# One block for all phases of a hybrid HGRN2 and gated-delta-net layer: a counted border, and three projection parts issued ahead of it

## The chip, the cores and the metric

The kernel runs on one core of a Trainium2 chip. The metric is the device time of one execution in microseconds (us), from start to end of the program. The kernel before takes 740.03 us, the median of three runs.

## What is computed

One decoder layer on 16 learned meta tokens and 1024 tokens of width 1024, in float32. In short:

```python
u = rmsnorm(h, norm_w)
proj = einsum('btd,dc->btc', u, w_in)           # 4096 columns + 8 gate columns
o_hg = causal_mixer(hgrn2_chunk, (q, k, v, logf), S0)              # 4 heads of 128
o_gd = causal_mixer(gdn_chunk, (gq, gk, gv, g, beta), S0g)         # 4 heads of 128, after a causal convolution of width 4
y = concatenate([gated_rmsnorm(o_hg, z_hg), gated_rmsnorm(o_gd, z_gd)])
h = h + einsum('btc,cd->btd', y, w_out)
out = rmsnorm(h, final_norm_w)[:, 16:]
```

`hgrn2_chunk` is a gated linear recurrence with a decay for each channel; `gdn_chunk` solves a lower triangular system in each chunk and carries a state from chunk to chunk.

## The kernel before, in words

**Tokens and heads.** The tokens are padded to 9 chunks of 128, in three groups g of three chunks. The normalised, transposed input stays in SBUF as a high and a low part (`uTh`, `uTl`), and each weight tile of 128 columns is split in the same way (`w_high` by ScalarE, `split_high`, L260; `w_low` by GpSimd, `split_low`, L268). A projection takes three products for each of 8 slices of the inner dimension.

**Phases.** The program runs nine phases: `front` (norm, transposes, gates and the first projection), then for every head h a delta-net phase `phase_gd(h)` (called gd0 to gd3 here) and an HGRN2 phase `phase_hg(h)` (hg0 to hg3). Each is a block of its own (`with nc.Block() as block`, L367, L1042, L1703), in which every engine has its own instruction stream. At the end of a block all engines meet at a barrier, and `end_block` (L192) clears the semaphores; the next phase uses the other half of them.

**The projection runs one step ahead.** While a phase works on its own head, TensorE projects what the next phase needs, so that TensorE always has work. A projection phase has 4 weight tiles of 3 token pieces, 12 pieces in all, and each piece is 8 parts (`project_part`, L241): 96 parts of three matmuls, numbered from 0. The steps of a phase each get some parts by a table (`give` in `phase_gd`, `parts` in `phase_hg`), and TensorE issues them behind the step's own matmuls. In hg3 the parts are those of the output product instead (`out_part`, L1099; 16 pieces of 6 parts, three matmuls of 512 columns each). Piece i is complete at part 8i+7, so piece 8 ends with part 71 and piece 10 with part 87.

**Who reads the table.** ScalarE, GpSimd and VectorE find their work on a piece by the step in whose parts the piece ends (`pieces`). ScalarE copies the piece out of PSUM (`take_hg`, L1715; `take_gd`, L1260), and behind pieces 2, 5 and 8 it splits the next weight tile. GpSimd does the low part at the same step in the gd phases:

```python
for key in order:
    ...
    take_low(pool, parts[key])            # pieces 2, 5, and 8 if more phases follow
    if key == ("blocks", 1):
        pool.wait_ge(m_in, 16)
        for g in range(NG):
            expand(pool, M, blk_m, g).then_inc(m_set, 1)
```

The steps of a gd phase are A1, A2 and A3 for each group (parts 0 to 31), `("blocks", 0)` (parts 32 to 41), `("blocks", 1)` (42 to 69), then for levels i = 4, 5, 6 `("B1", i)` with 3 parts and `("B2", i)` with 4, and `("end",)` with the last 5. Behind `("blocks", 1)` comes level 4: TensorE forms the product Y, ScalarE copies it, TensorE does the 3 parts of B1, and then forms Z = M Y (L2043), for which it waits for `m_set`, the three expansions of M by GpSimd (L1781). SyncE issues the weight tile that the third split of a gd phase needs (`load_weights(sp, 3, ...)`) behind the block moves of the triangular solve, `blk_m` among them.

In an hg phase the steps are `lead`, eight `gram` steps for each group, the `t` and `ty` steps at the end of a group (transposes), `rec` steps (the recurrence) and `end`. Transposing a group's normalised output (`ty`, L1606) waits for ScalarE's `normalise` (L1340) of that group. For the last group this is `turned`: it stands before the last part but one of `end` (L1638), and behind it only two parts are left.

Of the kernel before, what the change touches and what calls it, by code (L numbers as in the profile page):

```python
# [32 lines left out]
F32 = mybir.dt.float32  # L33
# [69 lines left out]
def hybrid_layer(nc, x, meta_tokens, norm_w, w_in, conv_w, lb_logits, hg_norm_w, A_log, dt_bias,  # L103
# [87 lines left out]

    def end_block():  # L192

        nonlocal mix_full, mix_free, raw_loaded, w_high, w_low, last_stored, piece_done, piece_out, eps_added
        nums = [s.num for s in sems.values()]
        nc.sync.sem_clear(range(min(nums), max(nums) + 1))
# [44 lines left out]
    def project_part(pe, n, kind, early=0):  # L241
# [10 lines left out]
        for k in range(part * per, (part + 1) * per):  # L252
            for i, (w, u) in enumerate(((wh, uh), (wh, ul), (wl, uh))):
                last = pe.matmul(acc[:, 0:tw], w[j % 2][:, k, :], u[:, k, t0:t0 + tw],  # L254
                                 start=(k == 0 and i == 0), stop=(k == KT - 1 and i == 2))
        if part == PARTS - 1:
            last.then_inc(piece_done, 1)

# [108 lines left out]
    with nc.Block() as block:  # L367
        x_in, rows_in, gate_in = [sem(f"x_in{i}") for i in range(XS)], sem("rows_in"), sem("gate_in")
        gate_high, gate_low, gate_done, gate_out = (sem(n) for n in ("gate_high", "gate_low", "gate_done", "gate_out"))
        const0, consts = sem("const0"), sem("consts")  # L370
        sq_done, rstd_done, scaled = sem("sq_done"), sem("rstd_done"), sem("scaled")
        cleared, u_high, ident_there = sem("cleared"), sem("u_high"), sem("ident_there")
        u_low = [sem("u_low_dve"), sem("u_low_pool")]
        lb_step, lb_exp = sem("lb_step"), sem("lb_exp")
        prm_in, blk_set = sem("prm_in"), sem("blk_set")
        ones_set, pm0, gate_step, mask_step, mask_set = sem("ones_set"), sem("pm0"), sem("gate_step"), sem("mask_step"), sem("mask_set")
        gate_exp, dec_sub, dec_exp = (sem(n) for n in ("gate_exp", "dec_sub", "dec_exp"))
        gam_stored, dec_in = sem("gam_stored"), sem("dec_in")
        tap0, conv_step, conv_done, silu = sem("tap0"), sem("conv_step"), sem("conv_done"), sem("conv_silu")

        @block.sync
        def _(sp):
            def load_x(i):
                sp.dma_start(xt[i % XS][:, :], x[0, (i - 1) * P:i * P, :]).then_inc(x_in[i % XS], 16)

            def load_tile(n, cols_):

                if n >= 2:
                    sp.wait_ge(w_low, n - 1)
                sp.dma_start(raw[(n - 1) % 2][:, :, :], cols_).then_inc(raw_loaded[(n - 1) % 2], 16)  # L390

            sp.dma_start(xt[0][0:META, :], meta_tokens).then_inc(x_in[0], 16)
            load_x(1)
            sp.wait_ge(cleared, 1)
            sp.dma_start(rows[0:48, :], conv_w.rearrange("l j (b c) -> (l j b) c", c=P)).then_inc(rows_in, 16)
            sp.dma_start(rows[48:56, :], norm_w.rearrange("l (b c) -> (l b) c", c=P)).then_inc(rows_in, 16)
            sp.dma_start(rows[56:64, :], lb_logits.rearrange("l (b c) -> (l b) c", c=P)).then_inc(rows_in, 16)
            sp.dma_start(rows[64:65, :], hg_norm_w).then_inc(rows_in, 16)
            sp.dma_start(rows[65:66, :], gdn_norm_w).then_inc(rows_in, 16)
            for i in range(2, XS):  # L400
                load_x(i)
            sp.dma_start(gate_raw[:, :, :], w_in_v[:, :, AB_COLS:AB_COLS + 2 * HEADS]).then_inc(gate_in, 16)
            for i in range(XS, NC):
                full(sp, front, ("x", i - XS, 1))
                load_x(i)
            load_tile(0, tile_cols("gd", GD_KINDS[0], 0))
            sp.dma_start(pr[:, 0, :], A_log[0:1, :].broadcast_to([P, HEADS])).then_inc(prm_in, 16)
            sp.dma_start(pr[:, 1, :], dt_bias[0:1, :].broadcast_to([P, HEADS])).then_inc(prm_in, 16)
            load_tile(1, tile_cols("gd", GD_KINDS[1], 0))
            load_tile(2, tile_cols("gd", GD_KINDS[2], 0))  # L410
            load_tile(3, tile_cols("gd", GD_KINDS[3], 0))
            load_tile(4, tile_cols("hg", 0, 0))
            freed(sp, front, "gam_rows")
            sp.dma_start(gam_dram, gamT[:, :]).then_inc(gam_stored, 16)
            sp.wait_ge(gam_stored, 16)
            load_decay(sp, 0, dec_in)
            load_tile(5, tile_cols("hg", 1, 0))
            sp.wait_ge(raw_loaded[0], 48)

        def rows_of(i):  # L420

            return META if i == 0 else P

        def low_part(eng, n):
# [3 lines left out]
            eng.wait_ge(u_high, n + 1)  # L428
            eng.tensor_tensor(ul[:, 4 * half:4 * half + 4, t0:t0 + w],
                              ut[n % 3][:, 0:4 * w].rearrange("p (k t) -> p k t", k=4),  # L430
                              uh[:, 4 * half:4 * half + 4, t0:t0 + w].bitcast(F32),
                              ALU.subtract).then_inc(u_low[n % 2], 1)

        @block.gpsimd
        def _(pool):
            pool.memset(neg_half[:, :], -0.5)
            pool.memset(ident[:, :], 0.0).then_inc(const0, 1)
            pool.memset(tri[:, :], 1.0).then_inc(const0, 1)
            pool.wait_ge(const0, 2)
            pool.affine_select(out=ident[:, :], in_=ident[:, :], compare_op=ALU.not_equal, fill=1.0,  # L440
                               base=0, pattern=[[-1, P]], channel_multiplier=1).then_inc(const0, 1)

            pool.affine_select(out=tri[:, :], in_=tri[:, :], compare_op=ALU.is_ge, fill=0.0,
                               base=0, pattern=[[1, P]], channel_multiplier=-1).then_inc(const0, 1)
            pool.wait_ge(const0, 4)
            pool.tensor_copy(mask_st[:, 0, :], ident[:, :]).then_inc(consts, 1)
            pool.memset(ones[:, :], 1.0).then_inc(ones_set, 1)
            pool.memset(pmask[:, :], 1.0).then_inc(pm0, 1)
            pool.wait_ge(pm0, 1)

            pool.affine_select(out=pmask[:, :], in_=pmask[:, :], compare_op=ALU.is_ge, fill=0.0,
# [33 lines left out]
            for i in range(AHEAD):  # L485
                rstd_tile(i)
# [1635 lines left out]
```

## Time and profile before

| | |
|---|---|
| median of 3 runs | 740.03 us (739.78 to 741.06) |
| profiled execution, device time | 739.73 us |
| its span, first to last instruction | 738.0 us |
| TensorE busy | 710.0 us, 96% of the span |
| VectorE, ScalarE, GpSimd busy | 449.6, 304.3, 350.5 us |
| mean granted TensorE clock | 0.996 of full speed |
| DMA | 44.94 MB, mean 61 GB/s |

All times of the trace are of one execution, whose device time is 1.7 us above its span. "Busy" of TensorE counts from a matmul's start to its modelled end, so that neighbours overlap: how fast TensorE goes is read from start to start. A name in brackets behind a row tells what ended the idle time before it; PEq, SPq and so on are the sequencers of the engines, POOL is GpSimd, DVE is VectorE, ACT is ScalarE, SP is SyncE, and PE is TensorE.

### The profile page before, as it was taken

What the parts mean: (1) busy time and instruction counts of PE and PEld (TensorE: products, weight loads), DVE (VectorE), ACT (ScalarE), POOL (GpSimd) and SP (SyncE); (2) the same over time, 40 slices, a digit from 0 to 9 for tenths busy, and PEclk for the clock granted to TensorE, in tenths of its full rate; (3) what the DMA queues carried; (4) which work ended last, traced back from release to release, by engine and by line L of the source; (5) the groups of instructions that cost most, each with busy time, mean ns of one, the idle gap of its engine ahead of it and who ended that gap; (6) DMA issues with size and microseconds to landing.
All of it is one profiled execution on the core that took longest, in us unless ns stands there. A gap on an engine that the chain in (4) does not pass through costs nothing. (4 is left out here: it accounts for less than half of the span.)

```text
span 738.0 us, 13493 instructions
## 1 busy us (share of the span) xinstructions
PE 710.0 (96%) x4852; PEld 678.4 (92%) x4852; DVE 449.6 (61%) x1017; ACT 304.3 (41%) x798; POOL 350.5 (47%) x462
## 2 busy tenths in 40 slices
PE   7999999999999999999999999999999999999995
PEld 6799999989999999999999999999999998788884
DVE  6854356379882562798924625989336158776247
ACT  6635423624553316345344154445442342232333
POOL 5782342167553322566624323767243456756423
PEclk9999999999999999999999999999999999999998
DMA  8355333130204226531548142102253324211005
GB/s 264 36 63 79 29 36 73 28 50 9 40 26 72 40 47 57 27 32 22 46 44 66 43 63 28 30 9 48 51 89 127 84 77 161 79 56 45 29 23 206
DMA packets 63990, 44.94 MB, mean 61 GB/s; under 512 B 17438, under 2 KB 59044, under 8 KB 63924
## 3 DMA queue, kind: packets, MB, share of 16 engines
q1 hardware_dynamic: 63924, 44.07, 33.3%
q8 instruction: 40, 0.66, 0.4%
q14 instruction: 26, 0.21, 0.1%
HBM read 35.82 MB, written 7.65 MB: 59 GB/s over the span
## 5 line engine op out<-in xcount | busy, mean ns | idle before, releaser
L254 PE MATMUL proj<-uTh,w_high 128*128 128x352 f32 (+4 forms) x768 | 261.3, 340 | 2.4 <-PEq L1703 2.4
L254 PE MATMUL proj<-uTh,w_low 128*128 128x352 f32 (+4 forms) x768 | 245.7, 320 | 0.0
L254 PE MATMUL proj<-uTl,w_high 128*128 128x352 f32 (+4 forms) x768 | 245.2, 319 | 0.0
L254 PEld LDWEIGHTS proj<-uTh,w_high 128*128 128x128 f32 x768 | 145.1, 189 | 3.3 <-issue 3.1
L254 PEld LDWEIGHTS proj<-uTl,w_high 128*128 128x128 f32 x768 | 145.1, 189 | 0.0
L254 PEld LDWEIGHTS proj<-uTh,w_low 128*128 128x128 f32 x768 | 144.2, 188 | 0.0
L272 POOL TENSOR_TENSOR w_low<-w_raw,w_high 128x256 fp32r<-128x256 f32 (+1 forms) x54 | 71.0, 1316 | 87.3 <-ACT w_high L264 40.0
L1221 POOL TENSOR_TENSOR f_suffix<-f_suffix,f_prefix 128x192 f32<-128x192 f32 x84 | 56.5, 672 | 34.0 <-DVE f_prefix L1429 27.2
L1623 PE MATMUL mix<-level_x 128*128 128x128 f32 x448 | 64.1, 276 | 1.1 <-DVE level_x L1420 0.8
L1623 PEld LDWEIGHTS mix<-level_x 128*128 128x128 f32 x448 | 60.5, 191 | 4.7 <-issue 2.8
L1439 DVE COPY_PREDICATED hg_scores<-mask_st,mix 128x384 f32<-128x384 uint8 (+1 forms) x96 | 52.0, 542 | 19.6 <-PE mix L1623 19.2
L1466 DVE SCALAR_TENSOR_TENSOR conv_out<-conv_in,hg_taps,conv_out 128x352 f32<-128x352 f32 (+2 forms) x81 | 50.9, 629 | 0.5
L1429 DVE TENSOR_TENSOR f_prefix<-f_prefix 128x192 f32<-128x192 f32 x84 | 48.0, 572 | 4.3 <-POOL f_suffix L1221 3.7
L1420 DVE TENSOR_TENSOR level_x<-hg_q,f_prefix 128x192 f32<-128x192 f32 (+1 forms) x84 | 48.2, 574 | 2.5
L1213 POOL TENSOR_TENSOR level_x<-hg_k,f_suffix 128x192 f32<-128x192 f32 (+1 forms) x72 | 45.4, 631 | 8.6 <-PE mix L1623 6.5
L876 ACT ACTIVATE gd_o<-mix,gd_cc 128x128 f32<-128x128 f32 x32 | 11.7, 366 | 74.4 <-DVE gd_r L866 74.4
L1109 PE MATMUL proj<-uTh,w_high 128*128 128x512 f32 x96 | 41.2, 429 | 0.7 <-PEq L1703 0.7
L1109 PE MATMUL proj<-uTh,w_low 128*128 128x512 f32 x96 | 37.9, 394 | 0.0
L1109 PE MATMUL proj<-uTl,w_high 128*128 128x512 f32 x96 | 37.8, 394 | 0.0
L2021 DVE COPY_PREDICATED gd_n<-mask_ts,mix 128x384 f32<-128x384 uint8 (+1 forms) x24 | 13.1, 546 | 39.0 <-PE mix L2043 38.4
L264 ACT CAST w_high<-w_raw 128x1024 fp32r<-128x1024 f32 x27 | 28.2, 1044 | 7.9 <-DMA w_raw<-in_w_in 6.7
L1201 POOL MEMSET f_suffix<- 128x384 f32 x12 | 5.7, 474 | 46.5 <-POOLq L1703 46.3
(301 smaller groups left out, 1381.4 us busy)
## 6 DMA issues: line engine op xcount, KB each, us to landing
w_raw<-in_w_in SPq DMA_DIRECT2D x32, 512.0 KB, 8.4
x_tile<-in_x SPq DMA_DIRECT2D x8, 512.0 KB, 6.6
w_raw<-y_scratch SPq DMA_DIRECT2D x8, 384.0 KB, 4.4
decay<-gamma_scratch SPq DMA_DIRECT2D x4, 576.0 KB, 3.7
landing<-in_w_out SPq DMA_DIRECT2D x4, 512.0 KB, 7.8
landing<-in_x SPq DMA_DIRECT2D x3, 512.0 KB, 6.4
out_y<-landing SPq DMA_DIRECT2D x3, 512.0 KB, 2.6
y_scratch<-gd_y SPq DMA_DIRECT2D x6, 192.0 KB, 1.8
```

Of the source, the lines that this page charges most:

```text
L254: last = pe.matmul(acc[:, 0:tw], w[j % 2][:, k, :], u[:, k, t0:t0 + tw], start=(k == 0 and i == 0), stop=(k == KT - 1 and i == 2))
L264: act.copy(wh[n % 2][:, :, :], raw[(n - 1) % 2][:, :, :]).then_inc(w_high, 1)
L272: last = pool.tensor_tensor(wl[n % 2][:, ks, :], raw[(n - 1) % 2][:, ks, :], wh[n % 2][:, ks, :].bitcast(F32), ALU.subtract)
L1109: last = pe.matmul(pbank[idx % 2][:, :], y[t % 2][:, k, :], wo_half(w, k, half), start=(k == 0 and i == 0), stop=(k == OUT_K - 1 and i == 2))
L1213: pool.tensor_tensor(xv_[:, :, 0, :], kv_[:, :, 0, :], sv_[:, :, 0, :], ALU.mult).then_inc(x_even, 1)
L1221: pool.tensor_tensor(sv_[:, :, 0, :], sv_[:, :, 0, :], pv_[:, :, 1, b - 1:b].broadcast_to([P, GW // (2 * b), b]), ALU.mult).then_inc(suf_d ...
L1420: dve.tensor_tensor(xv_[:, :, 1, :], qv_[:, :, 1, :], pv_[:, :, 1, :], ALU.mult).then_inc(x_odd, 1)
L1429: dve.tensor_tensor(pv_[:, :, 1, :], pv_[:, :, 1, :], pv_[:, :, 0, b - 1:b].broadcast_to([P, GW // (2 * b), b]), ALU.mult).then_inc(pre_do ...
L1439: dve.copy_predicated(A[g % 2][:, GC - n:GC, :], mask_st[:, m, :].unsqueeze(1).broadcast_to([P, n, P]), src).then_inc(bank_free(plan, ("gr ...
L1466: dve.scalar_tensor_tensor(out=out_, in0=cin[idx % 3][:, tap:tap + tw], scalar=cw[:, tap, kind:kind + 1], in1=out_, op0=ALU.mult, op1=ALU. ...
L1623: last = pe.matmul(ap[:, chunk(i)], left, right, start=True, stop=True)
L2021: dve.copy_predicated(part3(dst[:, gs]), msk.unsqueeze(1).broadcast_to([P, GC - lo, P]), src).then_inc(bank_free(plan, ("Z", i, g)), 1)
```

## The change

All phases now stand in one block. A semaphore `border` is never cleared; at the end of a phase each engine but TensorE drains and adds one to it (`leave`), TensorE's count is carried by a matmul, and at the start of a phase each engine waits until all five have counted (`meet`). TensorE issues three parts of the next phase's projection (`LEAD = 3`) before its own wait, and the first matmul of them carries its count. Every table of parts starts at 3 instead of 0, and the last step of each phase has three parts less. `clear_old` clears the old half of the semaphores in the next phase.

```diff
+    whole = ExitStack()
+    block = whole.enter_context(nc.Block())
+    border = ctx.enter_context(nc.semaphore("border", num=SEM_LO + 2 * SEM_HALF))
+    ENGINES, LEAD = 5, 3
+    old = []
+    def meet(eng):
+        if phase[0]:
+            eng.wait_ge(border, ENGINES * phase[0])
+    def leave(eng):
+        eng.drain().then_inc(border, 1)
+    def clear_old(sp):
+        if old:
+            sp.sem_clear(range(min(old), max(old) + 1))
...
+                if met is not None and n == 0 and k == 0 and i == 0:
+                    last.then_inc(met, 1)
...
+    def lead_in(pe, kind, low):
+        pe.wait_ge(w_low, low)
+        pe.wait_ge(piece_out, 4 * len(PIECES) - 1)
+        for n in range(LEAD):
+            project_part(pe, n, kind, met=border)
...
+    def out_lead_in(pe, low):
+        pe.wait_ge(w_low, low)
+        pe.wait_ge(piece_out, 4 * len(PIECES) - 1)
+        for n in range(LEAD):
+            out_products(pe, n, met=border)
...
-        parts, at = {}, 0
+        parts, at = {}, LEAD
         for key in steps:
-            n = {"lead": 4, "end": 10}.get(key[0], 4 if key[:2] == ("rec", NG - 1) else 2)
+            n = {"lead": 4, "end": 10 - LEAD}.get(key[0], 4 if key[:2] == ("rec", NG - 1) else 2)
...
-                turned = parts[("end",)][-2 if more else 8]
+            turned = parts[("end",)][-2]
...
                     if not more:
-                        if 2 <= n < len(steps) + 2:
-                            for idx in ends(parts[steps[n - 2]]):
+                    for lag in (2, 1):
+                        if lag <= n < len(steps) + lag and (lag == 1) == (steps[n - lag][:2] == ("rec", NG - 1)):
+                            for idx in ends(parts[steps[n - lag]]):
                                 take_out(dve, idx)
...
-        names, parts, at = [], {}, 0
+        names, parts, at = [], {}, LEAD
```

Every engine's function in every phase gets a `meet(...)` at its start and a `leave(...)` at its end (TensorE a `lead_in` or `out_lead_in` instead), and the `with nc.Block()` lines go.

Since a part keeps its number but moves three places up, a piece ends in an earlier step. The order of GpSimd in phase gd0 (the split of the weight tile is `w_low`, the expansion of M is `gd_m`), before:

```order
L272 TENSOR_TENSOR w_low<-w_raw,w_high 128x1024
L188 TENSOR_SCALAR gd_ss<-gd_ss 128x3
L190 TENSOR_TENSOR gd_rr<-gd_ss,neg_half 128x3
L1815 TENSOR_TENSOR gd_kd<-gd_kn,gd_cc 128x384
L1828 TENSOR_TENSOR gd_rr<-gd_ss,neg_half 128x9
L272 TENSOR_TENSOR w_low<-w_raw,w_high 128x1024 x2
L1781 TENSOR_TENSOR gd_m<-blk_m,blk_mask 128x384 x3
L272 TENSOR_TENSOR w_low<-w_raw,w_high 128x1024
```

and in the change:

```order
L318 TENSOR_TENSOR w_low<-w_raw,w_high 128x1024
L188 TENSOR_SCALAR gd_ss<-gd_ss 128x3
L190 TENSOR_TENSOR gd_rr<-gd_ss,neg_half 128x3
L1882 TENSOR_TENSOR gd_kd<-gd_kn,gd_cc 128x384
L1896 TENSOR_TENSOR gd_rr<-gd_ss,neg_half 128x9
L318 TENSOR_TENSOR w_low<-w_raw,w_high 128x1024 x3
L1845 TENSOR_TENSOR gd_m<-blk_m,blk_mask 128x384 x3
```

The third split stood behind the three expansions and now stands ahead of them, in gd0, gd1 and gd2 alike (gd3 has no third split here).

ScalarE in phase gd0 from piece 6 to level 4 (`hg_v` is the copy of pieces 6 to 8, CAST the split, `gd_xk` the copies of Y, `gd_m` those of the turned level), before:

```order
L283 ACTIVATE hg_v<-proj 128x352 x2
L1883 COPY gd_xk<-mix 128x256
L1883 COPY gd_xk<-mix 128x384 x2
L326 ACT_TABLE_LOAD
L326 ACTIVATE decay<-decay 128x384
L283 ACTIVATE hg_v<-proj 128x336
L264 CAST w_high<-w_raw 128x1024
L1893 COPY gd_m<-mix 128x256
L1893 COPY gd_m<-mix 128x384 x2
```

and in the change:

```order
L329 ACTIVATE hg_v<-proj 128x352 x2
L329 ACTIVATE hg_v<-proj 128x336
L310 CAST w_high<-w_raw 128x1024
L1953 COPY gd_xk<-mix 128x256
L1953 COPY gd_xk<-mix 128x384 x2
L372 ACT_TABLE_LOAD
L372 ACTIVATE decay<-decay 128x384
L1963 COPY gd_m<-mix 128x256
L1963 COPY gd_m<-mix 128x384 x2
```

Piece 8 and its split moved ahead of the copies of Y.

ScalarE in phase hg0 from piece 7 to piece 10 (`hg_vtok`, `hg_ktok` and `hg_on` are what is copied and normalised at `t` of the last group, `gd_z` are pieces 9 and 10, CAST the third split), before:

```order
L1360 COPY hg_vtok<-mix 128x384
L1361 COPY hg_ktok<-mix 128x384
L1340 ACTIVATE hg_on<-mix,hg_rs 128x128 x3
L1277 COPY conv_in<-proj 128x336
L1283 ACTIVATE conv_out<-conv_in,hg_taps 128x336
L1301 ACTIVATE gd_xq<-conv_out 128x352
L264 CAST w_high<-w_raw 128x1024
L1289 ACTIVATE gd_z<-proj 128x336
L1301 ACTIVATE gd_xq<-conv_out 128x336
L1332 ACTIVATE hg_sq,hg_ss<-mix 128x128 x3
L1289 ACTIVATE gd_z<-proj 128x352
L1340 ACTIVATE hg_on<-mix,hg_rs 128x128 x3
```

and in the change:

```order
L1335 COPY conv_in<-proj 128x336
L1341 ACTIVATE conv_out<-conv_in,hg_taps 128x336
L1359 ACTIVATE gd_xq<-conv_out 128x352
L310 CAST w_high<-w_raw 128x1024
L1419 COPY hg_vtok<-mix 128x384
L1420 COPY hg_ktok<-mix 128x384
L1399 ACTIVATE hg_on<-mix,hg_rs 128x128 x3
L1347 ACTIVATE gd_z<-proj 128x336
L1359 ACTIVATE gd_xq<-conv_out 128x336
L1347 ACTIVATE gd_z<-proj 128x352
L1391 ACTIVATE hg_sq,hg_ss<-mix 128x128 x3
L1399 ACTIVATE hg_on<-mix,hg_rs 128x128 x3
```

Piece 8 with its split moved ahead of the copies and of `hg_on` of the second group, and piece 10 (the second `gd_z`) ahead of the squares of the last group.

## Rows read from the trace of the kernel before

**Rows 1.** The page, part 1: busy time and share of the span of each engine

```profile
PE 710.0 (96%) x4852; PEld 678.4 (92%) x4852; DVE 449.6 (61%) x1017; ACT 304.3 (41%) x798; POOL 350.5 (47%) x462
```

**Rows 2.** Waits of TensorE: us in total, times, longest us

```profile
PE mix L849 <- ACT gd_u L880: 2.6, 6, 0.5
PE proj L254 <- PEq L1703: 2.4, 3, 0.8
PE mix L2041 <- PEq L1042: 2.4, 3, 0.8
...
PE mix L2041 <- PEq L367: 0.8, 1, 0.8
...
PE proj L1109 <- PEq L1703: 0.7, 1, 0.7
```

**Rows 3.** Timeline at the border gd0 to hg0: start us, us, engine, line, operation [idle before]

```profile
149.50 0.32 PE L254 MATMUL proj<-uTl,w_high 128*128 128x336 f32 x1
...
149.66 0.32 PE L254 MATMUL proj<-uTh,w_low 128*128 128x336 f32 x1
150.01 0.45 ACT L283 ACTIVATE hg_z<-proj 128x336 f32<-128x336 f32 x1 [3.25 <-PE proj L254]
...
150.77 0.41 PE L254 MATMUL proj<-uTh,w_high 128*128 128x352 f32 x1 [0.79 <-PEq L1703]
```

**Rows 4.** Timeline of phase gd0: SyncE, TensorE, GpSimd and ScalarE around its level 4

```profile
124.21 1.21 SPq L239 DMA_DIRECT2D w_raw<-in_w_in  x2
...
128.33 1.95 PE L2043 MATMUL mix<-gd_xk,gd_m 128*128 128x128 f32 x16
...
126.09 2.43 POOL L1781 TENSOR_TENSOR gd_m<-blk_m,blk_mask 128x384 f32<-128x384 f32 x3 [4.15 <-DMA blk_m<-blk_scratch]
...
131.99 2.36 POOL L272 TENSOR_TENSOR w_low<-w_raw,w_high 128x1024 fp32r<-128x1024 f32 x1 [3.47 <-ACT w_high L264]
...
130.86 1.05 ACT L264 CAST w_high<-w_raw 128x1024 fp32r<-128x1024 f32 x1 [1.06 <-DMA w_raw<-in_w_in]
```

**Rows 5.** The same in phases gd1 and gd2: TensorE and ScalarE

```profile
279.22 1.95 PE L2043 MATMUL mix<-gd_xk,gd_m 128*128 128x128 f32 x16
...
283.13 1.05 ACT L264 CAST w_high<-w_raw 128x1024 fp32r<-128x1024 f32 x1 [2.44 <-DMA w_raw<-in_w_in]
...
430.14 1.95 PE L2043 MATMUL mix<-gd_xk,gd_m 128*128 128x128 f32 x16
...
434.77 1.04 ACT L264 CAST w_high<-w_raw 128x1024 fp32r<-128x1024 f32 x1 [3.16 <-DMA w_raw<-in_w_in]
```

**Rows 6.** Windows at the end: stretch, PE busy, granted clock, DMA share, GB/s

```profile
729.00:730.00 1.00, 0.76 (x4) 1.00 0.27 106
...
732.00:733.00 1.00, 0.00 (x0) 0.72 0.47 184
```

**Rows 7.** Timeline of hg0 around the turn of the second group's output

```profile
215.53 0.83 PE L1623 MATMUL mix<-level_x 128*128 128x128 f32 x6
...
217.65 0.48 ACT L1360 COPY hg_vtok<-mix 128x384 f32<-128x384 f32 x1 [2.18 <-PE mix L1606]
...
219.34 0.55 PE L1606 MATMUL mix<-ident,hg_on 128*128 128x128 f32 x3
...
219.16 0.47 ACT L1277 COPY conv_in<-proj 128x336 f32<-128x336 f32 x1
...
220.61 1.04 ACT L264 CAST w_high<-w_raw 128x1024 fp32r<-128x1024 f32 x1
```

**Rows 8.** Timeline of hg0 around the turn of the last group's output

```profile
227.39 0.26 ACT L1332 ACTIVATE hg_sq<-mix 128x128 f32<-128x128 f32 x1
...
229.02 0.46 ACT L1289 ACTIVATE gd_z<-proj 128x352 f32<-128x352 f32 x1 [0.77 <-PE proj L254]
...
229.57 0.88 ACT L1340 ACTIVATE hg_on<-mix,hg_rs 128x128 f32<-128x128 f32 x3
...
231.60 0.49 PE L1606 MATMUL mix<-ident,hg_on 128*128 128x128 f32 x3
```

More of the change, by code:

```diff
@@ L366, in hybrid_layer @@
     AHEAD = 4
[L367 to L424, printed above, removed]
@@ L425, in low_part, with _, high_part @@
+    @block.scalar
+    def _(act):
+        meet(act)
+        def high_part(n):
             i, half = divmod(n, 2)
@@ new lines, in _ @@
+        early_high(3)
+        first_tap(1)
+        take_gd_front(act, 6, split=False)
+        take_gd_front(act, 7, split=False)
+        for g in range(NG):
+            decay_exp(act, g, dec_sub, dec_exp)
+        conv_end(0)
+        conv_end(1)
+        take_gd_front(act, 8, split=False)
+        early_high(4)
+        first_tap(2)
+        take_gd_front(act, 9, split=False)
+        take_gd_front(act, 10, split=False)
+        conv_end(2)
+        take_gd_front(act, 11, split=False)
+        leave(act)
@@ new lines, in phase_gd, with take_hg @@
+        dec_in, dec_sub, dec_exp = sem("dec_in"), sem("dec_sub"), sem("dec_exp")
+        if not more:
+            wo_in, wo_late, wo_high = sem("wo_in"), sem("wo_late"), sem("wo_high")
+        def take_hg(act, rng):
+            for idx in pieces(rng):
+                take_piece(act, kind, idx)
+                if not more and idx == Y_FREE - 1:
+                    y_split_high(act, 4, Y_FREE)
+                elif idx in (2, 5) or more and idx == 8:
+                    split_high(act, idx // 3 + 2)
@@ new lines, in _ @@
+        @block.gpsimd
+        def _(pool):
+            meet(pool)
+            pool.wait_ge(par, 1)
+            for g in range(NG):
+                scale_rows(pool, g)
+                if g == 1:
+                    split_low(pool, 1)
+            freed(pool, plan, ("qs", NG - 1))
+            pool.tensor_tensor(rr[:, 1, :], ss[:, 1, :], neg_half[:, 0:1].broadcast_to([P, NC]), ALU.pow
+                               ).then_inc(rq_done, 1)
+            for key in order:
+                if key == ("A1", 2):
+                    freed(pool, plan, ("qk", NG - 1))
+                if key == ("blocks", 1):
+                    pool.wait_ge(blk_turned, 1)
+                    if more:
+                        pool.wait_ge(dec_sub, NG)
+                take_low(pool, parts[key])
+                if key == ("blocks", 1):
+                    pool.wait_ge(m_in, 16)
+                    for g in range(NG):
+                        expand(pool, M, blk_m, g).then_inc(m_set, 1)
+            if not more:
+                wo_lows(pool, range(4))
+                y_split_low(pool, 4)
+            leave(pool)
@@ L1880, in _ @@
+                    decay_exp(act, i - BASE, dec_sub, dec_exp)
+                take_hg(act, parts[("B1", i)])
+                if not more and i < LEVELS - 1:
+                    wo_highs(act, ((0, 1), (2, 3, 4))[i - BASE])
+                if i < LEVELS - 1:
                     for g in range(NG):
```

2478 lines of the change are left out of this document (1254 added, 1224 removed).

## The prediction

> **What bounds the kernel now.** I read the page's busy shares first. TensorE is busy for 710.0 of 738.0 us and no other engine for more than 449.6 [rows 1]: the time is TensorE's instruction stream plus its gaps, and an edit counts by what it does to those gaps. Second, TensorE's own waits, to see which gaps there are. Eight of them are ended by a sequencer (PEq) and not by work: 2.4 + 2.4 + 0.8 + 0.7 us, the eight borders [rows 2]. The rest are short waits inside phases, the largest group being for ScalarE's `gd_u`, 2.6 us in six [rows 2]. Third, the timeline at one border, to see what such a gap is made of. The last matmul starts at 149.66, ScalarE takes the last piece from 150.01 to 150.46, and the first matmul of the next phase starts at 150.77 [rows 3]. From start to start that is 1.11 us, where two matmuls of a part are 0.155 to 0.16 us apart (149.50 to 149.66) [rows 3]. So a border costs TensorE 0.95 us, of which it is told "idle" for 0.79. Last, since the change moves every part three places against the steps, I read the timelines around those steps where a piece of the projection now ends earlier than what the engines have to do there.
>
> **The borders: gain.** Three lead parts are nine matmuls, 9 x 0.155 = 1.4 us. ScalarE's last copy ends at 150.46, 0.8 us after the last matmul's start, and a drain and a count add at most the 0.3 us that the barrier took from there to 150.77 [rows 3]; the others have finished earlier. So all have counted within 1.1 us and TensorE's wait behind the lead parts ends nothing. Gain: 7 x 0.95 and some 0.9 at the border to hg3 (the wait is 0.7 instead of 0.8 [rows 2]), together **-7.6 us**. Ends: 0, if the counted border costs as much behind the lead as the barrier did, and -8.5, if the slow first matmul behind a border (0.41 against 0.32 us [rows 3]) goes as well. `clear_old` and the drains lie on engines that are not late; I cost them at nothing, and with the cover of the lead gone they would cost no more than the border does now.
>
> **Level 4 of gd0, gd1 and gd2: loss.** Piece 8 ends with part 71. Before, part 71 stood in ("B1", 4) (parts 70 to 72); now ("blocks", 1) holds parts 45 to 72. With the piece, two things move ahead: ScalarE's split of the weight tile stands before the copies of Y, and GpSimd's low part stands before the three expansions of M. TensorE's Z of level 4 waits for these expansions one by one. Before they ran from 126.09 to 128.52 and Z started at 128.33, without a wait [rows 4]. Now they must wait for the low part, that for ScalarE's cast, and that for the tile's transfer, which SyncE issues only at 124.21, behind the block moves, and which ended ScalarE's wait at 130.86 [rows 4]. Nothing of this chain can start earlier, since the transfer is what it waits for. From the cast's start: 1.13 us to the low part's start (130.86 to 131.99), 2.36 us for it, 2.43 us for three expansions [rows 4], some 0.1 us to TensorE: 6.0 us. Z of the third group stands 10 matmul passes into the row of 16, 10 x 0.11 = 1.1 us after its start. So:
> - gd0: 130.86 + 6.0 = 136.9 against 128.33 + 1.1 = 129.4: 7.5 us [rows 4];
> - gd1: 283.13 + 6.0 = 289.1 against 280.3: 8.8 us [rows 5];
> - gd2: 434.77 + 6.0 = 440.8 against 431.2: 9.6 us [rows 5].
>
> Together **+25.9 us**. The lead puts both sides of each difference equally later, so it stays. TensorE is in order, so the parts behind Z cover nothing. Ends: the transfer takes 6.6, 8 and 8.7 us from its issue in the three phases, which is the spread I allow, 3 us up or down in all; and if the tile were there when piece 8 ends (about 125), only cast, low part and expansions would be late: 125 + 6.0 = 131 against 129.4, 1.6 us a phase.
>
> **TensorE's clock: loss.** Each of these waits leaves TensorE idle for six us and more at a stretch. At the program's end TensorE is last busy at 729.8 (0.76 of the window from 729), and the granted clock of 732 to 733 is 0.72: it has fallen from 2.4 to 1.2 GHz at about 732.4, after some 2.7 us of idleness [rows 6]. So each stall will end at the lower clock. How fast it comes back no row shows. The bounds: nothing, if it is back while Z still waits for the second and third expansion (1.6 us), and 3 us a phase, if the four parts of B2, the transposes and the next Y (some 5 to 6 us at full clock) all run at half. I take 1.5 us a phase, as long a return as the fall took with half of it lost, **+4.5 us**. The Trainium skill, "TensorE: Matmul & The Clock Gate", Part 1, states that the throttled clock is the default and that activity releases it; it speaks against this change wherever a stall is long. By that rule the sum has this term, 766.5; if the clock stayed up, it would be 762.
>
> **The hg phases: three moves.** (a) In hg0 to hg2 piece 8 and its split now stand before `hg_vtok`, `hg_ktok` and `hg_on` of the second group. Its first part follows the matmuls of 215.53, so the piece is there at 216.8. The copy-out to the end of the split takes 2.4 us (219.16 to 220.61, plus 0.95 to the next start), the copies and `hg_on` another 1.65 (217.65 to 219.3) [rows 7]: ready at 220.9, where TensorE turned it at 219.34 [rows 7]. +1.6 us a phase, **+4.8 us**. (b) At the last group's output part 87 now stands in the last `rec` step, three parts (1.4 us) earlier than 229.02, at 227.6, and ScalarE takes it before the squares. They start at 228.0; from them to the end of `hg_on` it is 3.06 us (227.39 to 229.57 + 0.88) [rows 8]: 231.1. TensorE wants it three parts earlier than 231.60, at 230.2 [rows 8]. +0.9 us a phase, **+2.8 us**. (c) Pieces 2 and 5 with their splits now fall on steps from which `gd_u` is two steps away instead of one; most of the 2.6 us of waits for `gd_u` should go [rows 2], by start-to-start 1.2 us a phase, **-3.7 us**. VectorE's convolution taps move by a step too; their waits are small, and I leave them at nothing, with 3 us either way for them and for hg3, whose pieces of six parts move by half a piece.
>
> **Sum.** 739.7 (the profiled execution's own time, 0.3 below the median) - 7.6 + 25.9 + 4.5 + 4.8 + 2.8 - 3.7 = 766.4, and with the 0.3 us to the median 766.7. I say **766.5 us**. Its own range is 759 to 774: 3 for the transfers, 4.5 for the clock, 3 for the hg phases, not all to one side.
>
> **Rivals.**
> - *The border only: faster.* GpSimd's third split does not hold the expansions. For that the tile would have to be in SBUF some 3.5 us before `blk_m` lands (126.09), before it is even issued (124.21) [rows 4]; so the place decides and the order of GpSimd speaks against it. It needs an error in my reading of which load the third split takes. Then 739.7 - 7.6 and the hg terms of 0 to +4: 732 to 736. Chance 0.04.
> - *The tile comes earlier.* If the third load were already there when piece 8 ends, level 4 would cost 1.6 us a phase, 4.8 in all, with no fall of the clock: 740 - 7.6 + 4.8 + 3.9 = 741. Between this and the forecast lie cases in which the transfers are quicker because others are spread, 745 to 758. Against it: SyncE's order is unchanged. Chance 0.06, of which 0.01 falls within 0.2% of before.
> - *The clock stays low long.* If TensorE's rate after each stall is halved through level 4 and into level 5, 6 us a phase go and the waits on TensorE behind it grow: 740 + 22 + 4 + 18 - 8 = 776 to 782. For it: the clock's fall is seen, its return is not. Chance 0.09.
> - *The change doesn't do what it says.* The lead parts are there, but one engine's count comes later than they cover, and the border costs its 0.95 us behind them: 774. Against it: SyncE and GpSimd are done long before, ScalarE 0.8 us after TensorE's last matmul [rows 3]. Chance 0.05.
>
> **How the numbers follow.** The forecast has 0.76. The range reaches from 757 to 777, which leaves out the faster rival, most of the early tile and the longest clock. About 0.2%, 1.5 us, is what a measurement of this kernel can tell from no change. Faster by more: 0.04. Within: 0.01. Slower by more: 0.95.
>
> **What would show it.** Right: TensorE's waits for a sequencer at borders gone; three waits of Z of 6 to 9 us each, ended by GpSimd's `gd_m`, with GpSimd in turn waiting for ScalarE's cast and that for the transfer; a granted clock of 0.5 in or behind them; new waits of TensorE for `hg_on`, 1.6 and 0.9 us, in hg0 to hg2; fewer for `gd_u`. Wrong: if Z starts without a wait, the greatest term falls, and the kernel is faster than before; if the clock stays at 1.0 through the stalls, 762; if the waits at borders are still there under the name `border`, that gain was none.

## The result, and the profile after

The change takes 765.0 us, the median of four runs (764.16 to 766.62), beside 740.54 us for the kernel before in the same comparison (739.78 to 741.48): a ratio of 1.0333, interval 1.032 to 1.0347. It is slower by 24.5 us, where 766.5 us was predicted with a range of 757 to 777. The profiled execution has a span of 763.9 us, 25.9 more than before, and a mean granted clock of 0.978 instead of 0.996.

The busy shares and the clock row of the page of the change:

```profile
PE 715.7 (94%) x4852; PEld 684.9 (90%) x4852; DVE 442.6 (58%) x1017; ACT 303.4 (40%) x798; POOL 350.4 (46%) x462
...
PEclk9999999799999997999999988999999999999999
```

The instructions are as many as before [rows 1]. TensorE is busy 5.7 us longer, and since no matmul was added, that can only be matmuls that ran slower. The clock row, 40 slices of 19 us each, dips at three places.

What TensorE waited for (us in total, times, longest):

```profile
PE mix L2117 <- POOL gd_m L1845: 24.1, 3, 8.5
PE mix L1670 <- ACT hg_on L1399: 7.0, 6, 1.6
...
PE mix L2117 <- DVE gd_n L1845: 1.0, 1, 1.0
```

Against [rows 2], every border wait and every wait for `gd_u` is gone, and three long waits of Z (L2117) for GpSimd's expansions and six for `hg_on` are new. The place of the first long one, phase gd0, by SyncE, ScalarE, GpSimd and TensorE:

```profile
126.87 1.21 SPq L258 DMA_DIRECT2D w_raw<-in_w_in  x2
...
133.78 1.04 ACT L310 CAST w_high<-w_raw 128x1024 fp32r<-128x1024 f32 x1 [7.79 <-DMA w_raw<-in_w_in]
...
134.90 2.34 POOL L318 TENSOR_TENSOR w_low<-w_raw,w_high 128x1024 fp32r<-128x1024 f32 x1 [10.27 <-ACT w_high L310]
137.20 2.43 POOL L1845 TENSOR_TENSOR gd_m<-blk_m,blk_mask 128x384 f32<-128x384 f32 x3
...
138.09 3.78 PE L2117 MATMUL mix<-gd_xk,gd_m 128*128 128x128 f32 x16 [7.49 <-POOL gd_m L1845]
```

This answers to [rows 4]: the weight tile lands 6.9 us after its issue, ScalarE splits it, GpSimd does its low part and only then the expansions, and Z starts 9.76 us later than before (128.33). Of this, 7.65 is the gap: from start to start behind the last matmul ahead of it (7.80 us), less the usual 0.155. Another 0.7 comes from the start of the program and some 1.2 from a wait for `gd_n` just before. The row of 16 matmuls takes 3.78 us where it took 1.95. The same in gd1 and gd2:

```profile
299.44 3.78 PE L2117 MATMUL mix<-gd_xk,gd_m 128*128 128x128 f32 x16 [8.13 <-POOL gd_m L1845]
...
460.19 3.78 PE L2117 MATMUL mix<-gd_xk,gd_m 128*128 128x128 f32 x16 [8.46 <-POOL gd_m L1845]
```

The windows around the stall of gd0 (stretch, length and TensorE busy, instructions, granted clock, DMA share, GB/s):

```profile
130.00:132.00 2.00, 0.61 (x4) 1.00 1.03 170
132.00:134.00 2.00, 0.00 (x0) 0.73 0.86 195
...
140.00:142.00 2.00, 2.00 (x11) 0.50 0.00 0
142.00:144.00 2.00, 2.00 (x11) 0.71 0.00 0
144.00:146.00 2.00, 2.00 (x20) 1.00 0.03 8
```

TensorE stops at 130.6, its clock goes from 2.4 to 1.2 GHz at about 132.9, and comes back at about 143.2, which is 5.1 us after Z began: 11 matmuls in 2 us at the low clock, 20 at the full one. (Here and below the moment is the share of a window that its mean leaves to each of the two levels.)

At the borders nothing is left. That from gd0 to hg0, as in [rows 3]:

```profile
160.66 0.32 PE L273 MATMUL proj<-uTh,w_high 128*128 128x352 f32 x1
...
160.81 0.32 PE L273 MATMUL proj<-uTl,w_high 128*128 128x352 f32 x1
...
160.86 0.45 ACT L329 ACTIVATE hg_z<-proj 128x336 f32<-128x336 f32 x1 [3.30 <-PE proj L273]
...
161.38 0.47 DVE L1455 COPY hg_fcur<-f_ab 128x2 f32<-128x2 f32 x1 [2.19 <-ACTq L205]
```

The matmul at 160.66 (352 columns) is the first of the lead; it comes 0.155 us behind the one before it, and the next two follow in the old rhythm of 0.155 to 0.16 us. VectorE (and GpSimd at 161.40) wait for ScalarE's count, TensorE does not.

Last, hg0: ScalarE before the turn of the second group's output, that turn, and the turn of the last group, as in [rows 7, 8]:

```profile
228.70 1.03 ACT L310 CAST w_high<-w_raw 128x1024 fp32r<-128x1024 f32 x1
...
230.38 0.90 ACT L1399 ACTIVATE hg_on<-mix,hg_rs 128x128 f32<-128x128 f32 x3
...
231.33 0.55 PE L1670 MATMUL mix<-ident,hg_on 128*128 128x128 f32 x3 [1.59 <-ACT hg_on L1399]
...
243.14 0.55 PE L1670 MATMUL mix<-ident,hg_on 128*128 128x128 f32 x3 [0.75 <-ACT hg_on L1399]
```

**Where the time went.** Take the phases between fixed points of TensorE's stream: from a delta-net phase's first transposes (L2115) to the next phase's first gram matmul (L1687), and on to the next transposes. Each such stretch has one border in it, worth 0.95 us, and so has the stretch from the start; only that of hg3 has none.

| stretch | before | after | difference |
|---|---|---|---|
| gd0, gd1, gd2 | 69.83, 69.85, 69.85 | 80.39, 79.13, 79.32 | +10.56, +9.28, +9.47 |
| hg0, hg1, hg2 | 81.03, 81.08, 80.92 | 81.79, 81.29, 81.28 | +0.76, +0.21, +0.36 |
| gd3 | 70.64 | 70.24 | -0.40 |
| hg3, gram to the last product of the layer | 101.06 | 96.21 | -4.85 |
| start to the first transposes | 82.95 | 83.67 | +0.72 |

Without the border's gain the stalls of gd0 to gd2 and the low clock behind them are 10.56 + 9.28 + 9.47 + 3 x 0.95 = 32.2 us. In the last three rows there is also work that changed stretches. The lead parts of gd0 now stand before its transposes (+1.4 in the last row). Those of hg3, nine matmuls of 512 columns, some 2.1 us, stand before its first gram matmul, so gd3 has 2.1 more and its own 1.4 less, and hg3 has 2.1 less; with a border that leaves hg3 a gain of its own of 2.75 us and gd3 of 0.1.

### The profile page after: what moved, and what is told of

Its sections match the earlier page's. It is cut to its first block, busy times and chain, and to the rows that moved or that the text cites. A ratio compares the mean times of both kernels' runs of the same rounds, so it can differ in the third digit from the quotient of the medians.

```text
span 763.9 us, 13440 instructions
## 1 busy us (share of the span) xinstructions
PE 715.7 (94%) x4852; PEld 684.9 (90%) x4852; DVE 442.6 (58%) x1017; ACT 303.4 (40%) x798; POOL 350.4 (46%) x462
## 3 DMA queue, kind: packets, MB, share of 16 engines
HBM read 35.82 MB, written 7.65 MB: 57 GB/s over the span
## 4 chain that ended last, share of the span: by engine, by line
PE 75%; DVE 9%; issue 7%; POOL 3%; ACT 2%; POOLq 2%; DMA 1%; SPq 1%; DVEq 0%; ACTq 0%
PE proj L273 35%; PE proj L292 8%; PE mix L2117 8%; PE mix L1687 6%; PE mix L1718 3%; PE mix L2115 2%; POOLq L205 1%; PE mix L1670 1%; PE mix L841 1%; DVE hg_scores L1500 1%; PE mix L890 1%; PE mix L825 1%; DMA blk_k<-blk_e 1%; POOL w_low L318 1%; PE mix L1664 1%
## 5 line engine op out<-in xcount | busy, mean ns | idle before, releaser
L1687 PE MATMUL mix<-level_x 128*128 128x128 f32 x448 | 64.1, 276 | 0.3
L1687 PEld LDWEIGHTS mix<-level_x 128*128 128x128 f32 x448 | 60.6, 191 | 4.0 <-issue 1.7
L1490 DVE TENSOR_TENSOR f_prefix<-f_prefix 128x192 f32<-128x192 f32 x84 | 45.0, 535 | 0.7 <-POOL f_suffix L1278 0.3
L2117 PE MATMUL mix<-gd_xk,gd_m 128*128 128x128 f32 x128 | 21.1, 333 | 24.1 <-POOL gd_m L1845 24.1
L2117 PEld LDWEIGHTS mix<-gd_xk,gd_m 128*128 128x128 f32 x128 | 20.0, 244 | 24.9 <-POOL gd_m L1845 24.9
```

What stands on the lines that cost most here:

```text
L1490: dve.tensor_tensor(pv_[:, :, 1, :], pv_[:, :, 1, :], pv_[:, :, 0, b - 1:b].broadcast_to([P, GW // (2 * b), b]), ALU.mult).then_inc(pre_do ...
L1687: last = pe.matmul(ap[:, chunk(i)], left, right, start=True, stop=True)
L2117: last = pe.matmul(ap[:, cs], left(i), right(i), start=True, stop=True)
```

## The experiments

All were compared with the kernel before on the same chip, whose median was 739.96 to 740.13 us in each comparison. Diffs are against the change, the first one's against the kernel before.

**The table alone.** The kernel before with its nine blocks; the tables start at 3, and TensorE does parts 0 to 2 right behind the barrier. It has everything of the change but the counted border and the lead ahead of it.

```diff
-        parts, at = {}, 0
+        parts, at = {}, 3
...
-            n = {"lead": 4, "end": 10}.get(key[0], 4 if key[:2] == ("rec", NG - 1) else 2)
+            n = {"lead": 4, "end": 7}.get(key[0], 4 if key[:2] == ("rec", NG - 1) else 2)
...
+                for n in range(3):
+                    project_part(pe, n, "gd") if more else out_part(pe, n)
                 project(("lead",))
```

> The blocks and barriers of before stay; only the tables move: TensorE does parts 0 to 2 right behind each barrier, every later step gets its parts as in the change, the last step three less. My theory says the loss is the table's alone and the border's gain is separate and adds: the change's time plus the 7.6 us of the eight borders, 771 to 774 us, with the same three waits of Z for gd_m (7.5 to 8.6 us) and the waits for hg_on. Rival, the loss comes from the new border (engines that now start at other times): 740 to 745 us and no long wait of Z.

Measured: 773.52 us (773.09 to 774.8), ratio 1.0454 (1.044 to 1.0468). Its waits of TensorE:

```profile
PE mix L2046 <- POOL gd_m L1784: 23.2, 3, 8.3
PE mix L1607 <- ACT hg_on L1340: 7.0, 6, 1.6
...
PE proj L254 <- PEq L1042: 2.4, 3, 0.8
```

The long waits are all there with the old borders, and the borders are still there too. The change is 8.5 us below this kernel, which is what its border and lead are worth: 8 borders of 0.95 us, and 0.1 for the slow first matmul behind each. The two halves of the change add up.

**The border alone.** One block and the counted border, but no lead: TensorE drains and counts like the others and then waits.

```diff
-    ENGINES, LEAD = 5, 3
+    ENGINES, LEAD = 5, 0
...
-        lead_in(pe, "hg", 5)
+        leave(pe)
```

> One block and the counted border, but LEAD = 0: no part ahead, TensorE drains and counts like the others, tables as before. My theory: what TensorE waits for at a border is mostly ScalarE's copy of the last piece (0.65 of the 0.95 us), so the counted border saves at most 0.3 us of each: 737.5 to 740.5 us, and a wait of TensorE of 0.5 to 0.8 us is left at each of eight borders. Rival, the block's barrier and branch are the cost: 732 to 734 us.

Measured: 738.75 us (738.34 to 739.4), ratio 0.9983 (0.9974 to 0.9991). TensorE's waits and its border gd0 to hg0:

```profile
PE mix L2114 <- ACTq L205: 2.3, 4, 0.6
...
PE proj L273 <- ACTq L205: 1.7, 3, 0.6
```

```profile
149.85 0.32 PE L273 MATMUL proj<-uTh,w_low 128*128 128x336 f32 x1
150.74 0.43 PE L273 MATMUL proj<-uTh,w_high 128*128 128x352 f32 x1 [0.57 <-ACTq L205]
```

From start to start a border is now 0.89 us instead of 1.11. So five counts on a semaphore are about 0.2 us cheaper than the barrier; the rest is ScalarE's last piece, which any meeting of the engines waits for. Of the gain at the borders the lead makes nearly all.

**One lead part instead of three.**

```diff
-    ENGINES, LEAD = 5, 3
+    ENGINES, LEAD = 5, 1
```

> The change with LEAD = 1. Piece 8 then ends in the step (B1, 4) again, as before, so GpSimd's third split stands behind the expansions, and in the hg phases pieces 8 and 10 stand where they did. My theory: no long wait of Z, no fall of the clock; one lead part covers 0.46 of the 0.95 us of a border, so 735 to 738 us. Rival, the loss grows with the parts that are moved (a third of it for a third of the lead): 745 to 750 us.

Measured: 733.18 us (732.4 to 734.68), ratio 0.9909 (0.9895 to 0.9922), 1.8 us better than the nearer end of what was expected. Its border:

```profile
149.82 0.32 PE L273 MATMUL proj<-uTh,w_low 128*128 128x352 f32 x1
150.24 0.43 PE L273 MATMUL proj<-uTh,w_high 128*128 128x352 f32 x1
```

One part, three matmuls, leaves only 0.26 us of the border's 0.95. The expectation had 0.46 us a border for the part and left out the 0.22 that the counted border itself gives; the two make 5.4 of the 6.9 us gained, and the waits for `gd_u` are 1.0 instead of 2.6 us. No piece crosses into another step that matters in gd0 to gd2 and hg0 to hg2: there is no wait for `gd_m` or for `hg_on`. In hg3 the trace has one new wait of TensorE, 1.9 us for VectorE's `gd_xv`. This edit of one number is faster than the kernel before by 6.9 us, where three parts are slower by 24.5.

**Two lead parts.** Does the loss grow with the lead, or does it come at a step?

```diff
-    ENGINES, LEAD = 5, 3
+    ENGINES, LEAD = 5, 2
```

> The change with LEAD = 2. ('blocks', 1) then holds parts 44 to 71, so piece 8 (part 71) still ends in it, by one part; in the hg phases pieces 8 and 10 also stand in the earlier steps. My theory, a step in the table decides and not the number of parts ahead: the whole loss is there again, three waits of Z for gd_m of 7 us and more, 762 to 769 us. Rival, the loss grows with the lead (733 at one part, 765 at three): 745 to 753 us.

Measured: 773.37 us (771.48 to 774.95), ratio 1.045 (1.0432 to 1.0468).

```profile
PE mix L2117 <- POOL gd_m L1845: 23.3, 3, 8.6
PE mix L1670 <- ACT hg_on L1399: 8.4, 6, 2.0
PE mix L890 <- DVE gd_o L951: 3.2, 4, 1.3
```

It is a step: `("blocks", 1)` holds parts 44 to 71 with a lead of 2, and 71 is the part that ends piece 8. But it is also 8.4 us worse than three parts, which neither theory had; 5.3 of them lie in the span (769.2 us), and the hg stretches alone have 6.4 more than those of the change. Piece 8 of an hg phase still stands ahead of `hg_on`, and now ends one part (0.46 us) later, so each wait there is 2.05 instead of 1.59 us. Two of these three waits also cost the clock. Windows of hg1:

```profile
390.00:391.00 1.00, 0.43 (x4) 0.96 0.00 0
391.00:392.00 1.00, 1.00 (x6) 0.50 0.06 16
...
394.00:395.00 1.00, 1.00 (x7) 0.84 1.01 77
```

The clock falls at 390.9, when TensorE has already been at work again for 0.35 us, and is back at 394.3. In hg2 it falls at 554.8, just as TensorE starts again, while in hg0 it stays at 1.00 behind a wait of the same 2.05 us. The stretches say what that costs: 82.57 us for hg0 against 84.13 and 84.08 for hg1 and hg2, **1.5 us for one fall of the clock**. The waits and this are 3 x 0.46 + 2 x 1.5 = 4.4 of the 6.4 us. Waits for `gd_o` and `gd_on` are 3.8 us more than in the change, 2.4 of them in hg0 to hg2 and 1.3 in hg3; what put them there was not tried.

**GpSimd's order back.** Only GpSimd's third split behind the expansions again; ScalarE's split stays ahead of the copies of Y.

```diff
-                take_low(pool, parts[key])
-                if key == ("blocks", 1):
+                if key != ("blocks", 1):
+                    take_low(pool, parts[key])
+                else:
+                    take_low(pool, [n for n in parts[key] if n // PARTS < 8])
                     pool.wait_ge(m_in, 16)
                     for g in range(NG):
                         expand(pool, M, blk_m, g).then_inc(m_set, 1)
+                    take_low(pool, [n for n in parts[key] if n // PARTS == 8])
```

> The change, but in the gd phases GpSimd does the low part of the third split behind the three expansions of M; ScalarE's order stays. My theory: Z then waits no more for gd_m but for ScalarE's copies of Y, which stand behind the cast that waits for the same transfer: 3.9, 5.3 and 6.0 us, with about 1 us of lost clock each, so 751 to 756 us. Rival, GpSimd's order is the whole loss and the transfer is hidden: 731 to 736 us.

Measured: 756.32 us (755.37 to 757.11), ratio 1.0215 (1.02 to 1.0231), 8.7 us below the change and 0.3 above the range that was expected. Z now waits for something else:

```profile
PE mix L2120 <- ACT gd_xk L1956: 15.8, 3, 5.8
```

```profile
133.13 1.04 ACT L310 CAST w_high<-w_raw 128x1024 fp32r<-128x1024 f32 x1 [7.19 <-DMA w_raw<-in_w_in]
134.09 1.13 ACT L1956 COPY gd_xk<-mix 128x256 f32<-128x256 f32 x3
...
134.59 3.75 PE L2120 MATMUL mix<-gd_xk,gd_m 128*128 128x128 f32 x16 [4.66 <-ACT gd_xk L1956]
```

The row of Z is as slow as in the change (3.75 us), since even this shorter stall takes the clock down. Two engines stood in the way of Z, one behind the other in what the profile names: undoing the one it names gives back 8.7 us, and lays bare the other.

**Both orders of the delta-net phases back.** As above, and ScalarE takes piece 8 behind the copies of Y of level 4.

```diff
-            take_hg(act, parts[("blocks", 1)])
+            held = parts[("blocks", 1)] if more else []
+            take_hg(act, [n for n in parts[("blocks", 1)] if n // PARTS < 8 or not held])
...
+                if i == BASE:
+                    take_hg(act, [n for n in held if n // PARTS == 8])
```

> The change, with both moves of the gd phases undone: GpSimd's low part behind the expansions, and ScalarE's piece 8 with its split behind the copies of Y. Lead and counted border stay. My theory: all of the gd phases' loss goes (32 us by the phases' lengths in the two traces, waits and clock together): 731 to 735 us, granted clock back at 0.996, no wait of Z. Rival, a part of the loss is the clock or the lead and stays: 738 us and more.

Measured: 735.72 us (735.33 to 737.39), ratio 0.9943 (0.9928 to 0.9958); it lies 0.7 us above what was expected, and the trace has 1.2 us of waits for `gd_o` that the change had not. The waits of Z are down to one of 0.8 us and the clock is 0.998:

```profile
PE mix L890 <- DVE gd_o L951: 1.8, 3, 0.6
...
PE mix L2123 <- ACT gd_xk L1957: 0.8, 1, 0.8
```

So 29.3 of the change's microseconds come from piece 8 in three phases.

**The hg phases back as well.** ScalarE takes pieces 8 and 10 where it took them before.

```diff
                 for idx in pieces(parts[key]):
+                    if idx in (8, 10):
+                        continue
                     take_gd(act, idx)
+                if key == ("t", NG - 1):
+                    take_gd(act, 8)
...
-            tail = pieces(parts[("end",)])
+            tail = [10, 11]
```

> As e5_gd_back, and in the hg phases piece 8 is taken behind hg_on of the second group and piece 10 behind the squares of the last group. My theory: the waits for hg_on (1.6 and 0.75 us in three phases) go, nothing else moves: 7 us below e5_gd_back, 724 to 728 us. Rival, a wait takes their place (VectorE's taps of piece 8 come later): 729 us and more.

Measured: 728.08 us (727.06 to 728.52), ratio 0.9833 (0.9819 to 0.9848). No wait for `hg_on` is left, and the step from 735.72 is 7.6 us, where 7 was expected. A second set of runs of the same kernel:

> The kernel of e6_all_back again, to be compared with the next one on the same chip with more rounds: 727 to 729 us.

Measured: 727.64 us (726.49 to 729.95), ratio 0.9836 (0.9821 to 0.9851), the same.

**The tile earlier.** The change with its orders as they are; SyncE issues the third split's tile behind the decay load, ahead of the block moves.

```diff
                 load_decay(sp, h + 1, dec_in)
+                load_weights(sp, 3, tile_cols("gd", GD_KINDS[0], h + 1))
             sp.wait_ge(blk_solved, 1)
...
             if more:
-                load_weights(sp, 3, tile_cols("gd", GD_KINDS[0], h + 1))
                 load_weights(sp, 4, tile_cols("gd", GD_KINDS[1], h + 1))
```

> The change with its orders on ScalarE and GpSimd as they are; only SyncE issues the third weight tile of a gd phase right behind the load of the decays, ahead of the block moves back, 14 us earlier. My theory: the transfer is the root of the chain. The cast then starts with piece 8, and cast, low part and expansion are late by 1.7 us a phase only, too short for the clock to fall: 736 to 741 us. Rival, the transfer is not what the chain waits for, or the tile now delays the block moves that Z needs as well: 750 us and more.

Measured: 739.54 us (738.46 to 743.13), ratio 0.9994 (0.9981 to 1.0008). Waits, and gd0:

```profile
PE mix L2117 <- DVE gd_n L1846: 2.7, 1, 2.7
PE mix L2117 <- POOL gd_m L1846: 2.2, 2, 1.1
```

```profile
125.71 1.04 ACT L310 CAST w_high<-w_raw 128x1024 fp32r<-128x1024 f32 x1
...
126.82 2.34 POOL L318 TENSOR_TENSOR w_low<-w_raw,w_high 128x1024 fp32r<-128x1024 f32 x1 [3.01 <-ACT w_high L310]
126.89 2.69 DVE L1846 TENSOR_TENSOR gd_n<-blk_n,blk_mask 128x384 f32<-128x384 f32 x1 [1.38 <-DMA blk_n<-blk_inv]
129.12 2.75 POOL L1846 TENSOR_TENSOR gd_m<-blk_m,blk_mask 128x384 f32<-128x384 f32 x3
```

With the same order of all compute engines 25.5 of the microseconds are gone, and the clock stays up (0.997). The order alone costs less: what made it dear is the transfer that ScalarE met at its place. The stretches of gd0 to gd2 are 71.81, 70.64 and 70.64 us here, 6.5 us in all above those of the kernel further below that has all orders back and the early tile (68.81, 68.81, 68.99). In gd0 TensorE waits 2.7 us for VectorE's `gd_n`, where it was 1.0 in the change. The block moves are not late there: VectorE starts its third `gd_n` at 126.89, earlier than in the change (127.67), but it takes 2.69 us instead of 0.56, while GpSimd's split of the tile runs beside it (126.82 to 129.16). In gd1 and gd2 the two don't meet and it takes 0.56.

**All orders back, and the tile earlier.**

> e6_all_back and e7_early_load together. My theory: with the orders restored nobody on the path waits for the tile, so the earlier load gives nothing: within 1 us of e6_all_back. Rival, ScalarE's wait for it (1 to 3 us a phase) still delays something on the path: 2 us or more faster.

Measured: 726.86 us (725.88 to 728.09), ratio 0.982 (0.9804 to 0.9836); and again, beside the second set without the early tile:

> The kernel of e8_all_back_early again. It was 1.2 us faster than e6_all_back, with intervals that overlap. If the earlier load takes away the waits of Z for ScalarE's copies and for gd_n that e6's trace shows (1.5 us in all), it is 1 to 2 us faster again; if that was scatter, the two are within 0.5 us.

Measured: 726.3 us (725.71 to 727.04), ratio 0.9815 (0.9802 to 0.9829). Twice this version was 1.2 to 1.3 us below the one with the tile at its old place, but the intervals overlap: that the early tile still gives something is likely, and not shown. In both traces with the early tile the waits of Z for ScalarE's copies of Y are gone, 0.9 and 1.0 us without it. The first of the two kernels was expected within 1 us of the one without the early tile, the second 1 to 2 us below it. It is the best version: 13.7 us faster than the kernel before, with the lead of three and with every engine's order as it was.

## Why the prediction was right

Its mechanisms were the ones that the traces show. That the total came within 1.5 us is partly luck, since two terms were off to opposite sides.

| step of the prediction | forecast | measured |
|---|---|---|
| borders | -7.6 | -7.6 from start to start, -8.5 with the slow first matmul; -8.5 as the change less the table alone |
| level 4 and the clock behind it, gd0 to gd2 | +25.9 + 4.5 = +30.4 | +32.2 by the stretches, 1.1 of it the wait for `gd_n` in gd0; +29.3 by undoing both orders |
| hg0 to hg2, their border left out | +4.8 + 2.8 - 3.7 = +3.9 | +0.76 + 0.21 + 0.36 + 3 x 0.95 = +4.2 |
| hg3 | 0 | -2.75 |

**The borders: right.** All waits at borders are gone and the first matmul behind one is as quick as any. The bound of 8.5 us, with that slow first matmul gained too, was the truer value: a border's first matmul was followed after 0.24 us in the kernel before and 0.27 with the counted border alone, and after 0.15 in the change.

**Level 4: right in mechanism and place.** The chain ran as worked out: tile, cast, low part, expansions, Z. From the cast's start to the end of the expansions it was 5.85 us in gd0 (133.78 to 137.20 + 2.43), and 6.0 with the way to TensorE had been forecast. The gap ahead of Z's first matmul was 7.65, 8.29 and 8.63 us (start to start, less the usual step). The forecast had 7.5, 8.8 and 9.6 for the third group's matmuls, 1.1 us into the row, which wait for the last expansion. With the 0.05 us to TensorE these expansions ended 8.1, 8.8 and 9.1 us behind the moment at which the third group would have started, 26.0 us in all, so the term of 25.9 was right. The experiment with the tile moved confirms the rival that was priced beside it: the prediction gave 741 us for a tile that is there in time, and it measured 739.54. The two are that close because that price left out both the wait of 2.7 us for `gd_n` and the gain of hg3 below.

A cost that the prediction did not have is about 1.1 us in gd0, the wait for `gd_n`. SyncE issued the block moves there 2.7 us later than before (`blk_m` at 126.36, not 123.69), 2 us more than the phase itself was late. These 2 us begin ahead of VectorE's solve, at the transfer of `blk_k`. Before:

```profile
107.49 1.91 SPq L1764 DMA_DIRECT2D blk_k<-blk_e  x3
...
110.62 0.17 DVE L1955 COPY blk_inv<-blk_k 72x8 f32<-72x8 f32 x1 [2.68 <-DMA blk_k<-blk_e]
```

and in the change:

```profile
108.21 1.91 SPq L1828 DMA_DIRECT2D blk_k<-blk_e  x3
...
113.31 0.17 DVE L2027 COPY blk_inv<-blk_k 72x8 f32<-72x8 f32 x1 [4.66 <-DMA blk_k<-blk_e]
```

From the issues to VectorE's first instruction it is 5.1 us instead of 3.1. In gd1 to gd3 of the change it isn't longer than before. Of the two profiled executions of the best version, which are of one kernel, one has the short time in gd0 and the other one 1.4 us more. So this term varies between executions; its cause is open.

**The clock: right, with its size at the edge of what is known.** It fell in each stall, and came back 5.1, 4.1 and 3.8 us after Z began. What that cost can be read against gd0 of the kernel with the early tile, where the clock stays up: from Z's first matmul to the next gram matmul it takes 23.50 us there, and 25.97, 25.54 and 25.40 in the change. The low clock costs TensorE 2.5, 2.0 and 1.9 us, 6.4 in all, half of the time for which it worked at 1.2 GHz. Part of this hides time that the forecast had under level 4, since at the full clock the row of Z would have waited some 0.5 us a phase for the last expansion. So the gaps and the clock come to 24.6 + 6.4 = 31.0 us, where 25.9 + 4.5 = 30.4 was forecast, and beyond the 26.0 above the clock's own share is some 5 us. With the 1.1 us for `gd_n` that is 32.1 of the 32.2 us. The value of 1.5 us a phase was a choice between bounds that no row of before could settle; the return took longer than the forecast had it, and the hidden 0.5 us brought the term near, which is luck. The Trainium skill, "TensorE: Matmul & The Clock Gate", Part 1, calls the throttled clock the default that activity releases; the trace agrees, 0.50 from 2.0 to 2.3 us into each stall and 1.00 again 3.8 to 5.1 us into the work behind it.

**The hg phases: right.** The wait for the second group's `hg_on` is 1.59 us in each of three phases, from start to start 1.75 (1.6 forecast). The last group's is 0.75 us, from start to start 0.92 (0.9 forecast). The waits for `gd_u` are gone altogether. Undoing (a) and (b) gave 7.6 us, and their sum was 7.6.

**hg3: the term that was mis-sized most.** It was put at nothing, within 3 us; it gained 2.75 us beyond the border. In the kernel before TensorE waited in that phase (its waits in the window of hg3, 606 to 708 us):

```profile
PE mix L843 <- DVE gd_r L866: 1.2, 1, 1.2
PE mix L859 <- ACT gd_on L921: 0.8, 1, 0.8
PE mix L834 <- DVE gd_o L895: 0.6, 1, 0.6
```

In the change none of the three is left there, and they are 2.6 us, as much as was gained. The gain comes with the table: the stretch from hg3's first gram matmul to the last product is as short with the table alone as in the change (96.2 us), and as long with the border alone (101.1) as before. VectorE takes the pieces of the output product in that phase, and they end half a piece earlier; that this is how the table takes the waits away is argued from the order, and no run isolates it.

**The sum.** -7.6 + 32.2 + 4.2 - 2.75 = 26.05 us, and the spans differ by 25.9; the forecast was 26.7. The terms that were off, +1.8 for the stalls and -2.75 for hg3, have opposite signs, so the total is nearer than its parts, and that is luck.

**The rivals.** "The border only" falls with the three waits of Z. "The tile comes earlier" falls for this change and is confirmed as a mechanism. "The clock stays low long" had 6 us a phase; it was 1.9 to 2.5. "The change doesn't do what it says" falls with the border's timeline.

## What to carry to other kernels

Where several engines find their work by a table of another engine's steps, moving the table by three places moves their instructions too: list, for each engine, which of its instructions changes sides with which, and for each ask whether what it waits for is there at the new place. Here two splits of a weight tile, each moved across three small operations, cost some 30 us because its tile was still in flight; keeping the order gave back 29.3 us, and issuing the tile earlier 25.5. A lead across a border needs only to be as long as the slowest engine's tail: here one part gained all but 0.26 us of a border and caused none of the long waits. And a wait that the profile names may have a second one just behind it, so that undoing the named one gives back only the difference.

## What was unexpected of the hardware

The clock of TensorE can fall for a stall that is already over. With a lead of two, three equal waits of 2.04 to 2.05 us came in hg0, hg1 and hg2; behind the first the clock stayed at 1.00, behind the other two it went to 0.50, in hg2 as TensorE started again and in hg1 0.35 us after, and stayed there for 3.4 us. Waits of 1.59 us never did it, three in the change and twelve more in four of the experiments; at the long stalls it fell after 2.3 us without a matmul in gd0, and after 2.0 in gd1 and gd2. The Trainium skill, "TensorE: Matmul & The Clock Gate", Part 1, says that the gate's watch on the engine runs freely and does not start anew with a kernel, which would explain that equal waits differ; no run here shows that cause.

A counted semaphore is hardly cheaper than the barrier at the end of a block: 0.89 against 1.11 us from start to start, 1.4 us over the whole program by the medians (738.75 against 740.13).

One VectorE instruction took two to five times its time beside one of GpSimd. The thirteen traces of this case have 156 of the `gd_n` instructions of 128x384 that read `blk_n`. The 117 that ran with no split of GpSimd beside them took 0.56 us each, and the 39 that ran beside one took 1.35 to 2.69 us, all but two of them 1.61 to 1.80. Such a meeting makes 2.1 of the 2.7 us that TensorE waited in gd0 with the early tile.
